# Cached values with the probabilities as the stationary operand, loaded ahead of the scans, in a two-layer hybrid decoder step

## The chip, the cores and the metric

One core of one Trainium2 chip runs the whole program. The metric is the device time of one execution in microseconds (us). The kernel before takes 2830.28 us (median of three runs, 2822.64 to 2831.82). TensorE is called PE, its weight loads PEld, VectorE DVE, ScalarE ACT, GpSimd POOL; SP only issues transfers.

## The reference

Two layers are run on 520 tokens: a prompt of 512 tokens and 8 sample tokens, each sample with a cache of 1024 positions, held as 8 pages of 128 positions that a page table points to. Per layer:

```
x = x + rms_post(Mix(rms_pre(x)))
x = x + rms_post2(ConvFFN(rms_pre2(x)))
```

`Mix` projects the normalised input once (29 tiles of 128 columns, and 32 tiles of gate logits) and feeds four branches: A, sparse attention (an indexer picks the top 256 of the 1025 keys of a sample, the top 128 of those of the prompt; 4 query heads, 2 key/value heads of 64), B, stick-breaking attention (4 heads of 64), C, an mLSTM scan, and D, a Mamba-2 scan. For a sample token, A and B need the products of 1024 cached probabilities and cached values for each head:

```
o = einsum('btjgn,btnjd->btjgd', p, v_sel)     # A, the selected ones, others have p = 0
o = einsum('bhtl,blhd->bthd', a, v)            # B
```

Each branch is projected, multiplied by the sigmoid of its gate logits and summed. `ConvFFN` follows with 44 up tiles and 22 down tiles.

## The kernel before, in words

**The ring.** Weights and cached pages come through four slots `R`. SP issues them in the order of the list `TILES`, and `tile_used` counts the tiles that PE is done with; a slot is loaded again when the tile four before is used. A cached unit is two pages: of keys 128 x 512 floats each (A's keys, two of B's, and the indexer's keys in 64 rows with zeros below), of values 128 x 384 each (128 of A, 256 of B). For each page the issuing engine first reads the page number out of `PT` into a register (`value_load`) and then issues the transfer (L403, L404, `cached`).

**The order in a layer.** First come 12 projections (L497), then the key stage (32 units; `rec` at L637 to L647): for each unit PE multiplies the indexer's queries `QI` (64 rows), A's queries `QA` (128 rows) and twice B's queries `QB` (128 rows) with the pages, each with 32 stationary columns and 256 moving ones, into partitions 0, 32 and 64. SP issues the units' pages and ACT those of the odd units from the fifth on. Then 17 projections, between which DVE selects the top 256 of the samples and PE, ACT and DVE do the other small steps. Then, in this order:

- sample probabilities of A transposed (L680, L682), copied by ACT into `PA` (L1079); 
- 12 groups of features turned token-major (PE L695, `TO_TM`), with ACT's evacuations (L1097) and the convolutions of D between them (DVE L1318, L1315); 
- cumulative sums (L706), row terms (L713), sample gates (L720), dots (L725 to L728), and eight steps for the samples' states (PE L742 and L746, POOL L1749 and L1755, DVE); 
- the scans of C and D: eight heads `v`, each with four blocks of key-query products (L776, L779), a broadcast (L758), decays on ACT (L1164, L1166), diagonals and weights on POOL, a product on DVE, and the state and output products on PE (L787 to L808);
- four blocks `t` of prompt queries for A and B (L842 to L895): the indexer's scores, the top-k on DVE for `t` of 1 to 3, softplus and sums for B, softmax for A.

**The fill.** The 32 gate tiles have no consumer before the branches are merged, so PE computes them (L582) in between. A step is 3 matmuls of 128 x 260, 16 steps are one tile. `fill(upto)` on PE, `drain(upto)` on ACT (which copies each half tile into `RB`, L1021) and `follow(upto)` on POOL run up to a given number of steps: `PRE` for the places ahead of the scans (96 steps), `LOOP` for the eight heads (64) and `IN_T`/`TO_T` for the four query blocks (352). SP stores each half from `RB` (L447, `keep`), and ACT may write `RB` again when the store has landed.

**Cached values before.** In head `v` of the scans PE multiplies the pages of sample `v` (L557, L562, `cached_values`), after the four key-query blocks of that head. The page is stationary, 128 x 128, and the probabilities move: 4 columns for A, 2 for each of B's two pairs. `MIX` puts the 32 value units into the list of tiles, four before each head's gate tiles, so they go through the ring:

```
mm(PS[:, 7, 448 + 4 * b:448 + 4 * b + 4], slot(l, n)[:, v0:v0 + 128],
   PA[:, 32 * j + 4 * b:32 * j + 4 * b + 4], start=j == 0, stop=j == 7,
   skip_group_check=True)
```

After the scans DVE adds and places the results (L1609 to L1617, signal `sa_out`), and PE waits for that in the first query block.

Of the kernel before, what the change touches and what calls it, by code (L numbers as in the profile page):

```python
# [11 lines left out]
NPR = 512  # L12
NSM = 8
TOK = NPR + NSM
HALF = TOK // 2
# [5 lines left out]
PAGES = 8  # L21
# [62 lines left out]
PRE = [0, 32, 48, 64, 72, 80, 96]  # L84
LOOP = [96 + STEPS * (v // 2 + 1) for v in range(8)]
SPENT = LOOP[-1]
IN_T = [[24, 16, 28, 12], [24, 16, 32, 14], [24, 16, 38, 14], [24, 16, 42, 12]]
TO_T = [[SPENT + sum(map(sum, IN_T[:t])) + sum(IN_T[t][:p + 1]) for p in range(4)] for t in range(NT)]
assert TO_T[-1][-1] == STEPS * NG

MIX = [("gate", q) for q in range(PRE[-1] // STEPS)]
for v in range(8):
    MIX += [("V", UPS * v + t) for t in range(UPS)]
    MIX += [("gate", q) for q in range((LOOP[v - 1] if v else PRE[-1]) // STEPS, LOOP[v] // STEPS)]
MIX += [("gate", q) for q in range(SPENT // STEPS, NG)]
TILES = ([("proj", c) for c in range(CUT)] + [("K", u) for u in range(NU)]
         + [("proj", c) for c in range(CUT, NPROJ)] + MIX + [("br", d) for d in range(KD)]
         + [("out", d) for d in range(KD)] + [("up", j) for j in range(2 * JF)] + [("down", t) for t in range(JF)])
AT = {tile: n for n, tile in enumerate(TILES)}

SPLIT_NEXT = [[q + 2] if AT["gate", q + 2] == AT["gate", q] + 2 else [] for q in range(NG - 2)] + [[], []]
IN_LOOP = [list(range((LOOP[v - 1] if v else PRE[-1]) // STEPS, LOOP[v] // STEPS)) for v in range(8)]
IN_LOOP[7] += [LOOP[7] // STEPS, LOOP[7] // STEPS + 1]
assert sorted([0, 1] + sum(SPLIT_NEXT, []) + sum(IN_LOOP, [])) == list(range(NG))

# [14 lines left out]
def trunk_kernel(nc, x_in, pages, consts, vecs, states, c_state, d_state, k_c, v_c,  # L120
# [9 lines left out]
    with ctx:  # L130
# [48 lines left out]
        QI = sb("QI", [64, NSM, 32])  # L179
# [4 lines left out]
        PA = QB[:, :, :, :].rearrange("p c b h -> p (c b h)")  # L184
# [30 lines left out]
        tile_used = sig("tile_used", NPROJ + 2 * NU + 40 + 8 + 44 + 22)  # L215
# [103 lines left out]
        sa_own = sig("sample_a_own_value", 1)  # L319
        sa_out = sig("sample_a_output", 1)  # L320
# [36 lines left out]
        for l in range(L):  # L357
            for n in range(tiles_per):
                at[(l * tiles_per + n) % RING] += 32 if TILES[n][0] in ("K", "V") else 16
                full_at.append(at[(l * tiles_per + n) % RING])  # L360
# [38 lines left out]
        def cached(eng, l, n, u, rec, src):  # L399

            eng.wait_ge(tile_used.sem, l * tiles_per + n - RING + 1)
            for j in range(2):
                pg = eng.value_load(PT[0:1, 2 * u + j:2 * u + j + 1], min_val=0, max_val=POOL - 1)  # L403
                eng.dma_start(slot(l, n)[:, rec * j:rec * (j + 1)],  # L404
                              src[l, bass.ds(pg, 1)].rearrange("o p c -> (o p) c")).then_inc(full(l, n)[0], 16)
# [5 lines left out]
        def _(sp):  # L411
# [14 lines left out]
            for l in range(L):  # L426
# [8 lines left out]
                for u in range(NU):  # L435
                    if not by_act(u):
                        cached(sp, l, AT["K", u], u, K_REC, k_c)
# [3 lines left out]
                def keep(n):  # L441

                    if TILES[n][0] == "gate":
                        q = TILES[n][1]
                        for a in range(2):
                            sp.wait_ge(*g_out.nth(l, 2 * q + a))
                            sp.dma_start(GATES[l, q, :, HALF * a:HALF * (a + 1)],  # L447
                                         RB[:, HALF * a:HALF * (a + 1)]).then_inc(g_stored[a].sem, 16)
                for kind, i in MIX:
                    n = AT[kind, i]  # L450
                    if kind == "V":
                        cached(sp, l, n, i, V_REC, v_c)
                    else:
                        tile(l, n, w_gate[l, i], 1024)
                    keep(n - RING)
# [1492 lines left out]
```

## Time and profile before

| what | value |
|---|---|
| median of three runs | 2830.28 us (2822.64 to 2831.82) |
| the profiled execution, its own time | 2841.91 us |
| its span, first to last instruction | 2839.8 us |
| mean granted clock of TensorE | 0.895 of full |
| PE busy | 89% of the span |
| DVE, ACT, POOL busy | 45%, 36%, 12% |
| DMA | 264.0 MB, 93 GB/s on the mean |

The page of the profile gives the busy time of each engine and the costliest groups of instructions. PEclk is the granted clock of TensorE as a share of its full speed (2.4 GHz; 0.5 is the lower level, 1.2 GHz). An idle time in brackets says how long the engine had been idle before the row, and who released it. Matmuls overlap, so the cost of one is read from start to start of neighbours rather than from its duration. The two layers are alike; a stage of the first one begins some 1407 us before that of the second.

### The profile page before, as it was taken

The page shows a single profiled execution, that of the slowest core. Times are in us where ns is not written, and L with a number is a line of the kernel's source. Part 1 is how long each engine was busy: PE and PEld are TensorE (multiplying, and loading weights), DVE is VectorE, ACT ScalarE, POOL GpSimd, SP SyncE. Part 2 cuts the span into 40 slices and gives each one's busy share as a digit, 9 for nine tenths or more (in the row PEclk, how much of TensorE's full clock was granted, in tenths as well). Part 3 has the DMA queues.
Part 4 walks back from the last instruction along what each step waited for, and adds up shares of the span by engine and source line. Part 5 has one row for each costly group of instructions (what it writes and reads, how often), then busy time and mean ns, then how long its engine had stood idle before and what let it go on. Part 6 is the DMA issues. An engine that isn't in the chain of part 4 may idle for free. (4 is left out here: it accounts for less than half of the span.)

```text
span 2839.8 us, 41630 instructions
## 1 busy us (share of the span) xinstructions
PE 2540.2 (89%) x16456; PEld 2175.6 (77%) x16456; DVE 1285.4 (45%) x2047; ACT 1013.4 (36%) x1526; POOL 348.1 (12%) x390
## 2 busy tenths in 40 slices
PE   6999679989999889999888997899899997999996
PEld 5659657767887789999885686477687776999895
DVE  3329341223556465662342383422234565666623
ACT  3123431224444345552230225222244433555521
POOL 0014232112320000000000132311222100000000
PEclk9999766769999899999999997676799998999998
DMA  3362112232326122222314422122322251222221
GB/s 151 111 201 90 58 47 77 77 100 68 89 75 196 60 67 91 97 91 82 103 60 148 156 75 68 58 68 83 92 79 89 84 172 52 83 97 90 88 84 60
DMA packets 111827, 264.00 MB, mean 93 GB/s; under 512 B 13458, under 2 KB 47250, under 8 KB 110738
## 3 DMA queue, kind: packets, MB, share of 16 engines
q1 hardware_dynamic: 99074, 238.25, 26.4%
q10 hardware_dynamic: 12560, 23.11, 2.4%
q8 instruction: 130, 2.13, 0.3%
q14 instruction: 63, 0.52, 0.1%
HBM read 233.71 MB, written 27.59 MB: 92 GB/s over the span
## 5 line engine op out<-in xcount | busy, mean ns | idle before, releaser
L497 PE MATMUL PS<-XH,WH 128*128 128x260 f32 x2592 | 540.2, 290 | 47.9 <-DVE XL L1315 36.3
L1003 ACT ACTIVATE WH<-R 128x1024 fp32r<-128x1024 f32 x270 | 286.0, 1059 | 780.5 <-PE PS L497 564.9
L497 PE MATMUL PS<-XL,WH 128*128 128x260 f32 x2592 | 529.2, 286 | 4.3 <-issue 2.8
L497 PE MATMUL PS<-XH,WL 128*128 128x260 f32 x2592 | 528.1, 285 | 0.0
L1339 DVE TENSOR_TENSOR WL<-R,WH 128x1024 fp32r<-128x1024 f32 x176 | 215.7, 1226 | 555.9 <-ACT WH L1003 555.6
L497 PEld LDWEIGHTS PS<-XH,WH 128*128 128x128 f32 x2592 | 408.6, 193 | 56.7 <-issue 43.7
L497 PEld LDWEIGHTS PS<-XL,WH 128*128 128x128 f32 x2592 | 406.3, 192 | 4.7 <-issue 4.7
L497 PEld LDWEIGHTS PS<-XH,WL 128*128 128x128 f32 x2592 | 405.7, 192 | 0.0
L582 PE MATMUL PS<-XH,WH 128*128 128x260 f32 x1024 | 304.8, 298 | 16.5 <-ACT RB L1021 16.3
L1714 POOL TENSOR_TENSOR WL<-R,WH 128x1024 fp32r<-128x1024 f32 x94 | 223.3, 2376 | 730.8 <-ACT WH L1003 729.9
L582 PE MATMUL PS<-XL,WH 128*128 128x260 f32 x1024 | 298.3, 291 | 0.0
L582 PE MATMUL PS<-XH,WL 128*128 128x260 f32 x1024 | 297.0, 290 | 0.0
L582 PEld LDWEIGHTS PS<-XH,WH 128*128 128x128 f32 x1024 | 202.4, 198 | 29.9 <-issue 22.2
L582 PEld LDWEIGHTS PS<-XH,WL 128*128 128x128 f32 x1024 | 202.1, 197 | 0.0
L582 PEld LDWEIGHTS PS<-XL,WH 128*128 128x128 f32 x1024 | 202.0, 197 | 0.0
L497 PE MATMUL PS<-FR,WH 128*128 128x260 f32 x1024 | 190.8, 289 | 8.9 <-issue 8.9
L497 PEld LDWEIGHTS PS<-FR,WH 128*128 128x128 f32 x1024 | 154.4, 195 | 9.7 <-issue 9.7
L1318 DVE SCALAR_TENSOR_TENSOR S<-S,V 128x510 f32<-128x510 f32 (+1 forms) x176 | 132.1, 751 | 44.9 <-ACT S L1282 41.8
L1021 ACT ACTIVATE RB<-PS 128x260 f32<-128x260 f32 x128 | 49.6, 387 | 246.8 <-PE PS L582 144.7
L915 PE MATMUL PS<-F,R 128*128 128x260 f32 x512 | 119.4, 388 | 4.5 <-DVE F L1315 3.1
L915 PEld LDWEIGHTS PS<-F,R 128*128 128x128 f32 x512 | 94.4, 190 | 29.1 <-DVE F L1315 9.8
L562 PE MATMUL PS<-QB,R 128*128 128x2 f32 x512 | 113.0, 325 | 0.0
(311 smaller groups left out, 3398.9 us busy)
## 6 DMA issues: line engine op xcount, KB each, us to landing
R<-w_up SPq DMA_DIRECT2D x88, 512.0 KB, 3.3
R<-w_gate SPq DMA_DIRECT2D x64, 512.0 KB, 3.7
R<-w_proj SPq DMA_DIRECT2D x58, 512.0 KB, 3.3
R<-v_c SPq DMA_DIRECT2D x128, 192.0 KB, 2.4
R<-w_down SPq DMA_DIRECT2D x44, 512.0 KB, 3.2
R<-k_c SPq DMA_DIRECT2D x72, 256.0 KB, 3.3
GATES<-RB SPq DMA_DIRECT2D x128, 130.0 KB, 3.7
S<-GATES SPq DMA_DIRECT2D x64, 260.0 KB, 2.7
```

Of the source, the lines that this page charges most:

```text
L497: i = mm(PS[:, bank + a, 0:HALF], p[:, w, k * 128:(k + 1) * 128], x[:, a * HALF:(a + 1) * HALF], start=first and p is WH and x is hi, stop ...
L562: ins = mm(PS[:, 7, o:o + 2], slot(l, n)[:, v0 + 128 + 128 * c:v0 + 256 + 128 * c], PA[:, 256 + 32 * j + 4 * b + 2 * c:256 + 32 * j + 4 * ...
L582: i = mm(PS[:, 1 + 2 * a, 0:HALF], p[:, half(l, m), k * 128:(k + 1) * 128], x[:, k, a * HALF:(a + 1) * HALF], start=k == 0 and p is WH and ...
L915: ins = mm(PS[:, 4 + 2 * (q % 2) + a, 0:HALF], slot(l, nb)[:, 256 * br + 128 * k:256 * br + 128 * k + 128], F[:, o + k, a * HALF:(a + 1) * ...
L1003: do(A(WH[:, half(l, m), :], slot(l, SPLIT[m]), ACT.Copy), w_hi)
L1021: do(A(RB[:, HALF * a:HALF * (a + 1)], PS[:, 1 + 2 * a, 0:HALF], ACT.Copy), g_out)
L1318: do(v_.scalar_tensor_tensor(out, a, sc, b, o0, o1), s)
L1339: v_.tensor_tensor(WL[:, half(l, m), :], slot(l, SPLIT[m]), WH[:, half(l, m), :].bitcast(f32), ALU.subtract).then_inc(w_lo.sem, 1)
L1714: g_.tensor_tensor(WL[:, half(l, m), :], slot(l, SPLIT[m]), WH[:, half(l, m), :].bitcast(f32), ALU.subtract).then_inc(w_lo_p.sem, 1)
```

## The change

The pages of values become the moving operand and the probabilities the stationary one. Four samples are handled side by side: for page `j` of samples `4 s` to `4 s + 3` (a quad, `k = 8 s + j`, 16 in a layer) PE issues four matmuls with 8 stationary columns and 384 moving ones, into partitions 0, 32, 64 and 96 of bank 0 or 2. Each matmul gives all 8 rows of probabilities (4 heads of A, 4 of B) against all 384 value columns, of which a head wants its own 64. ACT copies the bank out (`values_out`), PE picks the rows and turns them feature-major with three matmuls (`by_feature`), and DVE places the wanted parts. `PA` is laid out again, 8 probabilities of a page and sample side by side.

The quads do not pass the ring. They have two buffers of their own, `QUAD[0]` in `S` and `QUAD[1]` in the room of `TM` that D's features fill later; SP issues the four pages of quad `k` when quad `k - 2` is used. The first two quads are used after step 24 of the fill, and two more after each of the first seven token-major groups. `MIX` is gone: the gate tiles follow each other in the ring.

The fill is dealt out anew: 192 steps ahead of the samples' states (16 before A's sample probabilities are transposed, 12 behind each of seven token-major groups, and others), 4 in each of the eight state steps, 8 in each of the eight heads, and 224 in the query blocks. The exponential for A's samples moves behind the last projection. In the key stage `QI` has 128 rows, the lower 64 zeros, so that all four matmuls have the same shape.

The diff, cut to its core:

```
-PRE = [0, 32, 48, 64, 72, 80, 96]
-LOOP = [96 + STEPS * (v // 2 + 1) for v in range(8)]
-IN_T = [[24, 16, 28, 12], [24, 16, 32, 14], [24, 16, 38, 14], [24, 16, 42, 12]]
+LAST, PAST_P = 16, 24
+IN_TM = [36, 48, 60, 72, 84, 96, 108, 112, 120, 128, 136, 144]
+CUM, ROWS, SEL, DOTS = 160, 176, 184, 192
+IN_R = [DOTS + 4 * (s + 1) for s in range(8)]
+LOOP = [IN_R[-1] + 8 * (v + 1) for v in range(8)]
+IN_T = [[14, 10, 12, 10], [14, 10, 18, 12], [14, 10, 22, 14], [14, 10, 26, 14]]
...
+NQ = 16
+QUADS_AT = [PAST_P, PAST_P] + [IN_TM[i] for i in range(7) for _ in range(2)]
+LOAD_QUADS = [[k for k in range(NQ) if (QUADS_AT[k - 2] // STEPS + RING - 1 if k >= 2 else 1) == q] for q in range(NG)]
...
-        QI = sb("QI", [64, NSM, 32])
+        QI = sb("QI", [128, NSM, 32])
...
+        PA = QB[:, :, :, :].rearrange("p c b h -> p (c b h)").rearrange("p (n h) -> p n h", h=8)
+        QUAD = [buf[:, 0:4 * V_REC].rearrange("p (g c) -> p g c", g=4)
+                for buf in (S[:, 2:5, :].rearrange("p a t -> p (a t)"),
+                            TM[:, T_XX:T_XX + 4, :, :].rearrange("p a t d -> p (a t d)"))]
...
+                def cached_values(k):
+                    s, j = divmod(k, PAGES)
+                    if k == 0:
+                        sp.wait_ge(*sb_a.nth(l, 0))
+                    elif k >= 2:
+                        sp.wait_ge(*quad_used.nth(l, k - 2))
+                    for g in range(4):
+                        sp.dma_start(QUAD[k % 2][:, g, :],
+                                     v_c[l, bass.ds(page(sp, PAGES * (4 * s + g) + j), 1)].rearrange("o p c -> (o p) c")
+                                     ).then_inc(quad_full[k % 2].sem, 16)
+                for q in range(NG):
+                    tile(l, AT["gate", q], w_gate[l, q], 1024)
+                    if q >= RING:
+                        keep(q - RING)
+                    for k in LOAD_QUADS[q]:
+                        cached_values(k)
...
+            def cached_values(l, k):
+                s, j = divmod(k, PAGES)
+                pe.wait_ge(quad_full[k % 2].sem, 64 * (NQ // 2 * l + k // 2 + 1))
+                for g in range(4):
+                    ins = mm(PS[32 * g:32 * g + 8, 2 * s, 0:V_REC], PA[:, PAGES * j + 4 * s + g, :], QUAD[k % 2][:, g, :],
+                             start=False, stop=j == PAGES - 1, skip_group_check=True)
+                finish(ins, quad_used)
+            def by_feature(l, s):
+                pe.wait_ge(*sv_copied.nth(l, s))
+                pick = ident.rearrange("p (g r) -> p g r", g=4)
+                mm(PS[:, 2 * s, 384:400].rearrange("p (g h) -> p g h", g=4), PST[:, 0:128], pick[:, :, 0:4],
+                   start=True, stop=True)
+                for c in range(2):
+                    o = 400 + 8 * c
+                    ins = mm(PS[:, 2 * s, o:o + 8].rearrange("p (g h) -> p g h", g=4),
+                             PST[:, 128 + 128 * c:256 + 128 * c], pick[:, :, 4 + 2 * c:6 + 2 * c], start=True, stop=True)
+                finish(ins, sv_out)
...
-                    mm(PS[0:32, bank, col:col + 256], QI[:, b, :], rec[0:64, 3], start=st, stop=end,
+                    mm(PS[0:32, bank, col:col + 256], QI[:, b, :], rec[:, 3], start=st, stop=end,
...
+                fill(LAST)
                 pe.wait_ge(*sa_p.nth(l, 0))
...
+                fill(PAST_P)
                 pe.wait_ge(*sa_trc.nth(l, 0))
                 pe.wait_ge(*sa_own.nth(l, 0))
+                cached_values(l, 0)
+                cached_values(l, 1)
...
                     finish(ins, tm_done)
+                    fill(IN_TM[i])
+                    if i < 7:
+                        cached_values(l, 2 * i + 2)
+                        cached_values(l, 2 * i + 3)
+                    if i in (4, 9):
+                        by_feature(l, i // 5)
...
                         finish(ins, st_block)
-                    cached_values(l, v)
-
                     pe.wait_ge(*vu_ready.nth(l, v))
...
+                pe.wait_ge(*sa_out.nth(l, 0))
                 for i, c in enumerate([CQ, CQ + 1, CK, CK + 1, XC, XC + 1, XB, XB + 1]):
...
+                def values_out(s):
+                    act.wait_ge(*quad_used.nth(l, PAGES * s + PAGES - 1))
+                    if s:
+                        act.wait_ge(*sv_out.nth(l, 0))
+                    do(A(PST[:, 0:V_REC], PS[:, 2 * s, 0:V_REC], ACT.Copy), sv_copied)
...
+                    drain(IN_TM[i])
+                    if i in (3, 8):
+                        values_out(i // 5)
...
+                for s in range(2):
+                    dve.wait_ge(*sv_out.nth(l, s))
+                    o = OS[:, 16 * s:16 * s + 16]
+                    tt(o, o, PS[:, 2 * s, 384:400], ALU.add)
...
```

The four fills of a query block stand after the first products of A (`IN_T[t][0]`), after the sums of B (`[1]`), after the values of B (`[2]`) and after the last products of A (`[3]`).

## Rows read from the trace of the kernel before

**Rows 1.** The page of the profiled execution, busy times of the engines.

```profile
PE 2540.2 (89%) x16456; PEld 2175.6 (77%) x16456; DVE 1285.4 (45%) x2047; ACT 1013.4 (36%) x1526; POOL 348.1 (12%) x390
```

**Rows 2.** Busy times by stage, second layer: length, each engine, PEclk, DMA share, GB/s.

```profile
1522.00:1590.30 68.30, 60.08 (x290) 19.05 (x290) 0.50 (x3) 1.11 (x2) 0.00 (x0) 0.93 0.74 237
1709.00:1814.30 105.30, 76.52 (x414) 58.74 (x412) 50.03 (x96) 46.01 (x76) 28.02 (x17) 0.73 0.20 63
1749.00:1790.00 41.00, 27.23 (x182) 26.08 (x184) 10.45 (x36) 17.56 (x32) 7.89 (x6) 0.79 0.24 74
1790.00:1814.30 24.30, 20.49 (x32) 5.58 (x28) 21.06 (x19) 5.42 (x7) 13.00 (x9) 0.54 0.09 27
1814.30:2018.00 203.70, 190.84 (x860) 142.54 (x860) 39.76 (x60) 47.25 (x67) 43.42 (x102) 0.69 0.27 81
2036.00:2264.00 228.00, 220.62 (x1408) 181.83 (x1406) 103.54 (x261) 100.42 (x180) 57.96 (x56) 0.95 0.27 80
```

**Rows 3.** Same view, the eight stretches of cached values in the scans, second layer.

```profile
1828.36:1838.69 10.33, 10.33 (x50) 10.31 (x49) 0.46 (x2) 1.06 (x1) 2.88 (x3) 0.50 0.37 106
...
sum 71.37, PE 71.37 PEld 71.25 DVE 4.85 ACT 22.73 POOL 19.81; mean PE 8.92 PEld 8.91 DVE 0.61 ACT 2.84 POOL 2.48
```

**Rows 4.** Timeline of PE in the second stretch of cached values: start, duration, what.

```profile
1855.73 0.39 PE L557 MATMUL PS<-QB,R 128*128 128x4 f32 x2
...
1856.42 0.36 PE L557 MATMUL PS<-QB,R 128*128 128x4 f32 x2
...
1857.41 0.57 PE L557 MATMUL PS<-QB,R 128*128 128x4 f32 x2
...
1858.69 0.57 PE L557 MATMUL PS<-QB,R 128*128 128x4 f32 x2
```

**Rows 5.** The chain that ended last, second layer: start, duration, what.

```profile
1952.18 3.98 PE PS L803 x8
...
1957.34 5.88 PE PS L582 x48
...
2064.93 2.30 PE PS L879 x8
```

**Rows 6.** Timeline of PE, one unit of the key stage, first layer.

```profile
126.35 0.62 PE L637 MATMUL PS<-R,QI 64*32 64x256 f32 x2
126.90 0.40 PE L639 MATMUL PS<-R,QA 128*32 128x256 f32 x1
126.90 0.40 PE L647 MATMUL PS<-R,QB 128*32 128x256 f32 x1
...
127.88 0.62 PE L637 MATMUL PS<-R,QI 64*32 64x256 f32 x2
```

**Rows 7.** Busy times in the middle of the key stage, first layer.

```profile
130.00:180.00 50.00, 44.28 (x234) 14.60 (x233) 0.00 (x0) 0.00 (x0) 0.00 (x0) 1.00 0.86 275
```

**Rows 8.** Who PE waited for ahead of the scans, second layer: total, times, longest.

```profile
PE PS L706 <- DVE SMT L1315: 8.7, 1, 8.7
```

**Rows 9.** The same view inside the scans, second layer.

```profile
PE PS L758 <- DVE S L1315: 8.8, 3, 3.5
```

**Rows 10.** Timeline of SP's queue: two key pages; three value pages across two units.

```profile
1560.44 1.43 SPq L404 DMA_DIRECT2D R<-k_c  x2
...
1834.37 2.90 SPq L404 DMA_DIRECT2D R<-v_c  x3
```

**Rows 11.** DMA issues of cached pages: count, KB each, median us to landing.

```profile
R<-v_c SPq DMA_DIRECT2D x128, 192.0 KB, 2.4
```

**Rows 12.** Timelines of POOL, PE and DVE, last query block, second layer.

```profile
2217.39 1.37 POOL L1708 TENSOR_SCALAR_AFFINE_SELECT F<-F 128x128 f32<-128x128 f32 x4 [8.18 <-DVE F L1318]
...
2219.31 1.02 PE L866 MATMUL PS<-F,K 128*128 128x512 f32 x2
...
2245.41 0.15 DVE L1321 TENSOR_SCALAR MX<-MX 128x1 f32<-128x1 f32 x1
...
2250.81 1.98 PE L857 MATMUL PS<-F 64*128 64x512 f32 x4
```

More of the change, by code:

```diff
@@ L214, in trunk_kernel @@
         slot_full = [sig(f"slot{i}_full", 0) for i in range(RING)]
-        tile_used = sig("tile_used", NPROJ + 2 * NU + 40 + 8 + 44 + 22)
+        tile_used = sig("tile_used", NPROJ + NU + 40 + 8 + 44 + 22)
+        quad_full = [sig(f"value_pages{i}_loaded", 0) for i in range(2)]
+        quad_used = sig("value_pages_used", NQ)
         xt_ready = sig("normalised_ready", 16)
@@ L436, in _ @@
                     if not by_act(u):
-                        cached(sp, l, AT["K", u], u, K_REC, k_c)
+                        cached_keys(sp, l, u)
                 for c in range(CUT, NPROJ):
                     tile(l, proj(c), w_proj[l, c], 1024)
[L441 to L455, printed above, removed]
+                def keep(q):
+                    for a in range(2):
+                        sp.wait_ge(*g_out.nth(l, 2 * q + a))
+                        sp.dma_start(GATES[l, q, :, HALF * a:HALF * (a + 1)],
+                                     RB[:, HALF * a:HALF * (a + 1)]).then_inc(g_stored[a].sem, 16)
@@ L709, in _ @@
                 finish(ins, sm_cum)
-                fill(PRE[3])
+                fill(CUM)
                 pe.wait_ge(*sm_rt.nth(l, 0))
@@ L714, in _ @@
                 finish(ins, sm_tr)
-                fill(PRE[4])
+                fill(ROWS)
                 pe.wait_ge(*xbc_ready.nth(l, 5))
@@ L722, in _ @@
                 finish(ins, r_sel)
-                fill(PRE[5])
+                fill(SEL)
                 pe.wait_ge(*r_prod.nth(l, 0))
@@ L730, in _ @@
                 finish(ins, r_tr)
-                fill(PRE[6])
+                fill(DOTS)
                 for s in range(8):
@@ L748, in _ @@
                     finish(ins, r_bc)
+                    fill(IN_R[s])
                 pe.wait_ge(*sm_em.nth(l, 0))
@@ L1109, in _ @@
                     token_major(c)
-                token_major(7)
-                drain(PRE[1])
-                for i in range(8, len(TO_TM)):
+                for i in range(7, len(TO_TM)):
                     token_major(i)
-                drain(PRE[2])
                 act.wait_ge(*sm_v.nth(l, 0))
@@ L1149, in _ @@
                 do(A(S[0:8, 3, 0:512], PS[0:8, 2, :], ACT.Copy), r_trc)
-                drain(PRE[6])
+                drain(DOTS)
+                for s in range(8):
+                    drain(IN_R[s])
                 for c in range(2):
@@ L1733, in follow @@
                     while STEPS * (behind[0] + 1) <= upto:
-                        for nxt in SPLIT_NEXT[behind[0]]:
-                            split_rest(l, NPROJ + nxt)
+                        if behind[0] + 2 < NG:
+                            split_rest(l, NPROJ + behind[0] + 2)
                         behind[0] += 1
-                follow(PRE[4])
+                follow(DOTS)
                 pool.wait_ge(*r_trc.nth(l, 0))
```

119 lines of the change are left out of this document (45 added, 74 removed).

## The prediction

> **What bounds the kernel now.** The page comes first: PE is busy for 89% of the span, DVE for 45% [rows 1]. So PE's own work is the time, and an edit counts when it takes PE work out or moves PE's waits. Next come the busy times by stage [rows 2]: in the second layer the key stage lasts 68.3 us, the stretch ahead of the scans 105.3, the scans 203.7 and the query blocks 228.0. The reader is to see three things. PE is full in the scans (190.8 of 203.7) but granted 0.69 of its clock. Ahead of the scans it idles for 29 us, 8.7 of them in one wait for the log decays [rows 8]. In the query blocks it is full at 0.95. The changed instructions fill eight stretches of the scans, 71.4 us in all [rows 3], and the first of them runs at a granted clock of 0.50.
>
> The timeline shows why they are dear: a page (six records) takes 0.69 us from start to start while the clock is still full, and 1.28 us when it has fallen [rows 4]. Each record loads 128 columns for 2 or 4 moving ones. Here row and rule differ. By the Trainium skill, "TensorE: Matmul & The Clock Gate", section "LDWEIGHTS (loading the stationary operand)", 128 columns load in an estimated 107 ns. With it the 384 records of a layer would cost 41 us and the change would be worth 30 us less in a layer. The trace agrees at full clock alone (0.69 / 6 = 115 ns); at the lower level it shows 213 ns. I take the 71.4 us that were measured.
>
> **Prices.** A fill step is 5.88 us / 16 = 0.37 us [rows 5]. A record of 256 moving columns beside a partner in another column group is (127.88 - 126.90) / 4 = 0.245 us, and the two partners start in the same 10 ns [rows 6]. So a record of 384 columns is 0.37 us, and a quad (two records, four groups side by side) 0.73 us; one after another it would be 2.9 us. Four groups at once are not shown; two are, so I take 0.73. SP's two pages back to back take 1.43 us, the second issue itself 0.33, so 1.10 us from page to page; three pages across a unit's wait take 2.90, so 1.47 for the one behind the wait [rows 10]. A quad costs SP 4 x 1.10 + 0.37 = 4.8 us, and a gate's tile and two stores are three more issues of 0.33 us and a little, 1.25 us together. A page lands 2.4 us after its issue [rows 11].
>
> **The scans.** Out go 71.4 us. PE waits 8.8 us for DVE in three places [rows 9]; two of them (3.5 each) lie in heads that had no fill behind them and now have 8 steps: 5.8 less. In two heads (v = 2 and 4) the fill halves from 16 steps to 8 and no longer covers ACT's root and DVE's reciprocal ahead of the next product: 2.4 more each, 4.8, my estimate. Clock: the output products take 3.98 us behind a cached stretch and 2.30 for the same columns in the query blocks [rows 5]; eight heads could give 13 us there and some more on the small ones, but heads with waits fall back, so I take 10. The fill stays 64 steps. Sum -82, between -62 (no clock gain, all waits opened) and -95.
>
> **Ahead of the scans.** The fill grows from 96 to 224 steps here. In order:
> - To the second quad: 24 steps 8.8, transposes and the opening of two banks 2, two quads 1.5: 12.3 us.
> - The seven groups with two quads each. PE's own work is 84 steps 30.9, 14 quads 10.2, transposes and picking 6.6: 47.7 us. SP has 14 quads at 4.8 (66.8) and five gates at 1.25 (6.3), and the last landing 2.4: 75.5 us. With two buffers SP can't run ahead: quad k waits for quad k - 2. So **SP's issuing sets the pace**, 10.8 us for a group, and PE idles some 3 us in each. Behind the waiting SP stand the gate stores and gate tiles; the tiles have a ring of four and the stores a gate's length, so I add nothing. The bytes are no bound: 1.6 MB in 10.8 us is 146 GB/s, beside 275 in the key stage [rows 7].
> - Five more groups: 36 steps 13.2, the rest 5: 18.2.
> - From the decays to the dots: 48 steps as before, and the 8.7 us wait stays, since ACT starts that chain when the fill ahead of it is drained. 41, as in the trace [rows 2].
> - The state steps took 24.3 us, DVE busy for 21.1 of them [rows 2]; 32 steps (11.8) lie in their gaps in part: 32.
>
> Sum 179 against 105: +74. The bounds are +46 (SP costs nothing) and +84 (quads one after another, which makes PE's group 11 us and adds waits). ACT's two copies, DVE's 18 small placings and the move of A's exponential lie behind fills of 16 steps and more: 0; if that cover fails it is about 3 us.
>
> **Query blocks.** 128 steps fewer: -47. But the fills covered other work. In the last block POOL's mask ends at 2217.39 + 1.37 = 2218.76 and PE takes it at 2219.31, and DVE's chain before POOL is fixed [rows 12]. With 10 steps fewer (3.7 us) PE waits 3.1 us. Over four blocks this point gives some 10 us, the second fill (6 steps fewer against a slack near 1.2) 4, and in the last block the maximum is ready at 2245.6 while PE, which came at 2250.81, would now come near 2243: 2.5. So +16, sum -31, between -20 and -47.
>
> **Key stage.** The index products, of another shape, run alone for 0.55 us of a unit's 1.53 [rows 6]. With 128 rows they can join the others: 0.98. But the transfers are 86% busy at 275 GB/s in the middle of the stage [rows 7], and 28 units of 0.52 MB take 53 us at that rate. I take -5, between -13 (DMA always busy) and +10 (the gaps let the clock fall, and a unit takes twice 0.98).
>
> **The sum.** -82 + 74 - 31 - 5 = -44 us in a layer, -88 in two. The profiled execution took 2841.9 us (span 2839.8), which is 11.6 above the median of the runs; 2841.9 - 88 = 2754, and against the median **2742 us**.
>
> **The rivals.**
> - *SP's issuing is hidden.* Then the seven groups take PE's 47.7 us, 28 less in a layer: 2686. This is what a rule gives too. By the Trainium skill, "DMA: Bandwidth & Descriptors", section "Issuing engines are not separate DMA queues", the sequencer's time to start a DMA is usually small beside the DMA. Against it: at 275 GB/s a page of 0.197 MB needs 0.7 us and SP 1.10 [rows 7, 10]. For it: PE's waits let SP catch up. 0.12.
> - *The scans give back only the matmuls.* The clock stays low in heads full of small products and the waits open: 62 instead of 82, 2782. For it: 0.69 of the clock now [rows 2]. 0.17.
> - *Quads one after another.* 10 us more in a layer, 2762. Against it: the pair that starts together [rows 6]. 0.10.
> - *The key stage doesn't pack.* Its part of the change does nothing: 2752. 0.06.
> - *Slower: the idle times ahead of the scans and in them drop the clock for all fills there.* 288 steps at 0.71 us instead of 0.37 cost 98 us in a layer, of which SP's pace hides 28; the 10 us of clock gain go too. That is +80, so 2902 us. It decides from the point where over half of these steps run slow (44 of 80). Against it: the stretch ahead of the scans idled for 29 us and still had 0.73 [rows 2]. 0.06.
>
> The forecast has 0.49, with a range of its own of 2710 to 2775. The cases between 2675 and 2795 hold 8 in 10, once the bounds of the scans and of the groups are taken in; outside lie the slower case and the far ends. About 0.3% (8 us) is what a measurement can tell from no change. Faster 0.91, within it 0.03 (part of the clock case), slower 0.06.
>
> **What would show it.** Right: no PE rows of 128x2 and 128x4 in the scans, that stage near 120 us; in the groups SP's page rows 1.1 us apart without gaps, and PE waiting about 3 us for them in each; four rows of 8 columns that start together; new waits of 1 to 3 us ahead of L866's counterpart; the key stage near 60 us with DMA its main wait. Wrong: a stretch ahead of the scans of about 150 us (SP hidden) or over 200; a scan stage over 140; fills at 0.71 us a step through whole groups; or index products that still start alone.

## The result, and the profile after

The changed kernel takes **2884.0 us** in the median of four runs (2878.9 to 2886.5) where the kernel before takes 2830.7: 1.9% slower, a ratio of 1.0192 with a 95% interval of 1.0168 to 1.0217. The forecast was 2742. The profiled execution took 2882.1 us with a span of 2878.8; that is 39 us over the span of before, whose profiled execution was itself 11 us above its median.

First the page's busy times, for [rows 1].

```profile
PE 2418.3 (84%) x15976; PEld 2059.0 (72%) x15976; DVE 1289.5 (45%) x2065; ACT 1015.8 (35%) x1530; POOL 347.9 (12%) x390
```

PE has 122 us less to do, and the kernel is slower: over 160 us of idle time are new. The stages of the second layer say where (busy times by stage, for [rows 2]: key stage; all that lies ahead of the scans; of it the seven groups and the state steps; scans; query blocks. Columns: length, PE, PEld, DVE, ACT, POOL, PEclk, DMA share, GB/s).

```profile
1545.90:1607.40 61.50, 42.37 (x290) 18.18 (x290) 0.00 (x0) 0.00 (x0) 0.00 (x0) 0.80 0.78 254
1726.70:1929.20 202.50, 153.29 (x943) 120.72 (x943) 55.20 (x118) 58.48 (x98) 49.00 (x26) 0.78 0.40 118
1739.50:1820.00 80.50, 57.17 (x417) 43.10 (x417) 22.34 (x40) 25.17 (x43) 11.85 (x5) 0.83 0.65 187
1881.70:1929.20 47.50, 41.40 (x129) 24.65 (x129) 18.13 (x20) 2.22 (x4) 16.09 (x11) 0.61 0.06 17
1929.20:2080.20 151.00, 110.06 (x454) 66.09 (x453) 40.01 (x57) 50.27 (x71) 38.96 (x100) 0.75 0.07 21
2098.80:2303.00 204.20, 176.30 (x1029) 135.38 (x1027) 102.00 (x260) 86.63 (x158) 39.04 (x48) 0.95 0.18 57
```

| stage of a layer, us | before | forecast | after |
|---|---|---|---|
| key stage (mean of both layers) | 66.3 | 61.3 | 64.0 |
| seven groups with quads | - | 75.5 | 80.5 |
| the rest ahead of the state steps | - | 71.5 | 74.5 |
| state steps | 24.3 | 32 | 47.5 |
| scans | 203.7 | 122 | 151.0 |
| query blocks | 228.0 | 197 | 204.2 |

The stages from the state steps on hold most of the error: 15.5 us in the state steps, 29 in the scans, 7 in the blocks. (The last 8 of the scans' 64 fill steps, 3 us, lie behind the end of this stage in the changed kernel and inside it in the kernel before, so like for like the scans take 154 us.) The waits of PE name the places. Who PE waited for in the scans, for [rows 9], and then in the state steps (total, times, longest):

```profile
PE PS L811 <- DVE F L1350: 18.8, 4, 9.0
PE PS L808 <- DVE F L1350: 17.4, 3, 9.0
PE PS L790 <- ACT F L1201: 3.8, 1, 3.8
...
PE PS L773 <- POOL F L1785: 6.3, 1, 6.3
PE PS L777 <- POOL F L1791: 6.1, 1, 6.1
```

The wait of 6.3 us ahead of L773 ends at 1881.74, just where the state steps begin; the one of 6.1 lies in them. In the scans PE waits 6 to 9 us in every other head. Three of these four waits (7 to 9 us) stand where a gate has just ended; the fourth, 6.0 us in the first head, has another cause (POOL itself waits there 7.7 us for ACT's decays) and is there in the kernel before too, with 5.1 us ahead of L776, in a line of the view of [rows 9] that is not shown there. DVE is only the last link; the timeline of all engines at one of the three places has the first (start, duration, engine and line, operation; in brackets the idle time before and who ended it).

```profile
2021.53 1.06 ACT L1031 ACTIVATE WH<-R 128x1024 fp32r<-128x1024 f32 x1
2022.74 2.34 POOL L1750 TENSOR_TENSOR WL<-R,WH 128x1024 fp32r<-128x1024 f32 x1 [33.19 <-ACT WH L1031]
2025.15 1.38 POOL L1744 TENSOR_SCALAR_AFFINE_SELECT F<-F 128x128 f32<-128x128 f32 x4
2026.60 0.92 POOL L1805 COPY U<-F 128x1 f32<-128x1 f32 x4
2027.62 2.06 POOL L1807 TENSOR_SCALAR S<-TM,U 128x64 f32<-128x64 f32 x4
2029.77 1.27 DVE L1350 TENSOR_TENSOR F<-F,PS 128x512 f32<-128x512 f32 x2 [9.41 <-POOL S L1807]
2030.51 1.65 PE L811 MATMUL PS<-F 128*128 128x256 f32 x4 [8.98 <-DVE F L1350]
```

It is read from the bottom. PE's third block (L811) waits for DVE's product, DVE for POOL's weights (L1807). POOL had stood idle for 33.19 us: the next item in its queue was the low part of a gate's weights (L1750), which needs ACT's leading part (L1031), and ACT makes that only when PE has ended the gate two before. So the order is: fill ends, ACT copies and splits, POOL makes the low part (2.34), and only then the next head's diagonals and weights (4.5), DVE, PE. In the kernel before, POOL's queue had the same order, a low part ahead of the next head's weights, and POOL idled for 27 us ahead of it. There ACT made the leading part as soon as the gate's tile had landed, in the middle of a head, under 10 us of cached values [rows 3] and with a fill still to come. POOL and DVE at such a place of the kernel before:

```profile
1890.26 2.34 POOL L1714 TENSOR_TENSOR WL<-R,WH 128x1024 fp32r<-128x1024 f32 x1 [27.09 <-ACT WH L1003]
1895.13 2.05 POOL L1770 TENSOR_SCALAR S<-TM,U 128x64 f32<-128x64 f32 x4
...
1909.42 1.27 DVE L1315 TENSOR_TENSOR F<-F,PS 128x512 f32<-128x512 f32 x2
```

The next head's weights are done at 1897.18, and DVE's product comes 12 us later. The change takes the cover away and ties the leading part to the end of a fill.

**Theory 1**: POOL's queue, as told. **Theory 2**: the fills run at a low clock in the state steps and scans (0.61 and 0.75), and PE would be the bound there even without the waits. **Theory 3**: SP's issuing sets the seven groups.

### The profile page after: what moved, and what is told of

Same layout as the page of the kernel before. It is cut to its first block and busy times, and to the rows that moved or that the text cites. A ratio compares the mean times of both kernels' runs of the same rounds, so it can differ in the third digit from the quotient of the medians.

```text
span 2878.8 us, 40698 instructions
## 1 busy us (share of the span) xinstructions
PE 2418.3 (84%) x15976; PEld 2059.0 (72%) x15976; DVE 1289.5 (45%) x2065; ACT 1015.8 (35%) x1530; POOL 347.9 (12%) x390
## 5 line engine op out<-in xcount | busy, mean ns | idle before, releaser
L514 PE MATMUL PS<-XH,WH 128*128 128x260 f32 x2592 | 540.4, 290 | 46.9 <-DVE XL L1350 35.1
L1031 ACT ACTIVATE WH<-R 128x1024 fp32r<-128x1024 f32 x270 | 286.0, 1059 | 723.6 <-PE PS L514 567.7
L514 PE MATMUL PS<-XL,WH 128*128 128x260 f32 x2592 | 528.4, 285 | 3.5 <-ACT WH L1031 3.5
L514 PE MATMUL PS<-XH,WL 128*128 128x260 f32 x2592 | 528.9, 286 | 0.0
L514 PEld LDWEIGHTS PS<-XH,WH 128*128 128x128 f32 x2592 | 409.2, 193 | 55.5 <-issue 44.1
L514 PEld LDWEIGHTS PS<-XL,WH 128*128 128x128 f32 x2592 | 405.8, 191 | 3.9 <-issue 3.9
L514 PEld LDWEIGHTS PS<-XH,WL 128*128 128x128 f32 x2592 | 406.5, 192 | 0.0
L601 PE MATMUL PS<-XH,WH 128*128 128x260 f32 x1024 | 319.4, 312 | 28.5 <-ACT RB L1049 24.6
L1750 POOL TENSOR_TENSOR WL<-R,WH 128x1024 fp32r<-128x1024 f32 x94 | 223.5, 2378 | 900.8 <-ACT WH L1031 899.7
L601 PE MATMUL PS<-XL,WH 128*128 128x260 f32 x1024 | 307.7, 300 | 0.0
L601 PE MATMUL PS<-XH,WL 128*128 128x260 f32 x1024 | 306.3, 299 | 0.0
L601 PEld LDWEIGHTS PS<-XH,WH 128*128 128x128 f32 x1024 | 212.0, 207 | 66.9 <-issue 53.8
L601 PEld LDWEIGHTS PS<-XL,WH 128*128 128x128 f32 x1024 | 212.1, 207 | 0.0
L601 PEld LDWEIGHTS PS<-XH,WL 128*128 128x128 f32 x1024 | 211.9, 207 | 0.0
L1353 DVE SCALAR_TENSOR_TENSOR S<-S,V 128x510 f32<-128x510 f32 (+1 forms) x176 | 132.1, 751 | 44.3 <-ACT S L1317 40.9
L656 PE MATMUL PS<-R,QI 128*32 128x256 f32 x128 | 53.7, 532 | 52.1 <-DMA R<-k_c 42.5
```

What stands on the lines that cost most here:

```text
L514: i = mm(PS[:, bank + a, 0:HALF], p[:, w, k * 128:(k + 1) * 128], x[:, a * HALF:(a + 1) * HALF], start=first and p is WH and x is hi, stop ...
L601: i = mm(PS[:, 1 + 2 * a, 0:HALF], p[:, half(l, m), k * 128:(k + 1) * 128], x[:, k, a * HALF:(a + 1) * HALF], start=k == 0 and p is WH and ...
L656: mm(PS[0:32, bank, col:col + 256], QI[:, b, :], rec[:, 3], start=st, stop=end, skip_group_check=True)
L1031: do(A(WH[:, half(l, m), :], slot(l, SPLIT[m]), ACT.Copy), w_hi)
L1353: do(v_.scalar_tensor_tensor(out, a, sc, b, o0, o1), s)
L1750: g_.tensor_tensor(WL[:, half(l, m), :], slot(l, SPLIT[m]), WH[:, half(l, m), :].bitcast(f32), ALU.subtract).then_inc(w_lo_p.sem, 1)
```

## The experiments

### One thing in another order (e1_late_rest)

POOL makes a gate's low part one step or one head later, behind the next head's weights. The gate needs it 16 fill steps on, so nothing new waits.

```
-                follow(DOTS)
+                follow(SEL)
...
-                    follow(IN_R[s])
+                    follow(IN_R[s - 1] if s else DOTS)
...
-                    follow(LOOP[v])
+                    follow(LOOP[v - 1] if v else IN_R[7])
+                follow(LOOP[7])
```

> Edit: POOL makes a gate's low part (2.35 us) one head, or one state step, later: behind the next head's weights in place of ahead of them. Nothing else differs from the changed kernel (2884 us). Theory 1 (POOL's queue: the low part stands ahead of the next head's diagonals and weights, so the state products come about 9 us after the fill): PE's waits in the scans of the second layer for VectorE and ACT (18.8 + 17.4 + 3.8) fall under 15 together and the stage goes from 151 to about 120 us; the state steps lose their two waits of 6 us and go from 47.5 to 38 to 44; together 35 to 40 us in a layer, so 2804 to 2815 us. Theory 2 (the low clock of the fills in these stages, the waits are only where the slack shows): PE stays the bound there, the fills slow down as the waits go, less than 12 us in a layer, so over 2860 us. Theory 3 (SP's issuing in the groups): no difference, 2884.

Measured: **2785.9 us**, 98 less than the changed kernel and 0.9842 of the kernel before (0.9794 to 0.9889). Busy times of its state steps and scans, second layer, and what is left of PE's waits in the scans:

```profile
1820.50:1858.90 38.40, 35.42 (x128) 21.94 (x128) 17.92 (x19) 2.22 (x4) 18.49 (x12) 0.69 0.13 38
1858.90:1981.30 122.40, 103.57 (x454) 61.90 (x453) 39.23 (x58) 50.28 (x71) 39.00 (x100) 0.82 0.09 26
```

```profile
PE PS L808 <- DVE F L1350: 8.4, 2, 6.0
PE PS L790 <- ACT F L1201: 6.3, 1, 6.3
PE PS L811 <- DVE F L1350: 3.1, 2, 2.6
```

The scans take 122.4 us, the state steps lose 9 and the dots ahead of them 4 (the wait of 6.3 us falls to 1.7). These are 42 us in a layer, the other 7 are spread over quads, key stage and blocks; I had expected 35 to 40 in all. One reason: the granted clock of the scans rises from 0.75 to 0.82 as the waits go, and PE's busy time falls by 6.5 us for the same instructions. In the state steps 6.0 of the 9 us are PE's busy time, at 0.61 before and 0.69 now. What is left of the waits that were to fall under 15 us is 17.8; 12.3 of it stand in the first head, the 6.0 us ahead of L808 from above and 6.3 ahead of L790, and are no matter of POOL's order. The same place as above, in this kernel:

```profile
1942.98 0.92 PE L811 MATMUL PS<-F 128*128 128x256 f32 x4
1943.06 1.06 ACT L1031 ACTIVATE WH<-R 128x1024 fp32r<-128x1024 f32 x1
...
1944.26 2.35 POOL L1750 TENSOR_TENSOR WL<-R,WH 128x1024 fp32r<-128x1024 f32 x1 [11.78 <-ACT WH L1031]
```

POOL does the same 2.35 us at the same moment, but PE is past L811 already. Theory 1 holds.

### The fill in the state steps (e9_no_state_fill, e7_late_no_state_fill)

The 32 fill steps of the state steps go to the query blocks, with the low part where the change has it, and with it late.

```
-IN_R = [DOTS + 4 * (s + 1) for s in range(8)]
+IN_R = [DOTS] * 8
...
+IN_T = [[18, 12, 14, 10], [18, 12, 20, 12], [18, 12, 24, 14], [18, 12, 28, 14]]
```

> Edit: the changed kernel (low part where it was, ahead of the next head's weights) without fill in the state steps, their 32 steps in the query blocks. With the late low part this moved the state steps from 38 to 28 us, the scans from 122 to 115 and gave 28 us in all (2786 to 2758). If the two causes (POOL's order, fill at half clock in the state steps) are independent: the state steps fall from 47 to about 28 (both waits of 6 us are gone with the fill as well), the scans stay at 143 to 151, the blocks take 2 to 8 more, 2840 to 2855 us. If the state steps' waits come back in the scans' first heads: over 2860.

> Edit: the low part a head later, and no fill in the eight state steps: their 32 steps go to the query blocks, 8 to each. In the run with the late low part alone the state steps take 38.4 us and the fill there runs at half clock (2.9 us for four steps). If the fill at half clock is what makes them long: the steps fall to the 24 of the kernel before, 14 less, and the blocks take 32 x 0.37 = 12 more less the 3 to 8 us of waits that they cover: 2770 to 2785 us. If the clock of the state steps costs nothing beyond their work, no gain: 2786 or more.

| time, us | fill in the state steps | none |
|---|---|---|
| low part as in the change | 2884.0 | 2822.3 |
| low part late | 2785.9 | 2757.6 |

The two causes are not independent: the late low part gives 98 us with this fill in place and 65 without it. e9 is at 0.9968 of the kernel before (0.9952 to 0.9983), 18 us better than the best that I expected: its state steps fall from 47.5 to 25.5 us and the scans from 151 to 145.7, and the blocks take 205.4 in place of 204.2. e7 is at 0.9733 (0.9694 to 0.9773), 12 us under the range expected of it: the state steps fall to 28.2 and 28.1 us (24 expected), and the scans give 6 and 10 more, the 10 in the second layer, where PE's wait of 6.3 us ahead of L790 is gone. In e1 ACT had stood at the state steps' last gate copy and split, with the output gates and the first head's decays behind it. Why the fill is dear there is in the groups of instructions of the changed kernel, the fill's leading product first in the state steps, then in the scans (count, busy, mean ns):

```profile
L601 PE MATMUL PS<-XH,WH 128*128 128x260 f32 x32 | 13.5, 423 | 0.0
...
L601 PE MATMUL PS<-XH,WH 128*128 128x260 f32 x57 | 16.9, 296 | 0.0
```

One takes 423 ns there against 296. From start to start it is plainer: in six of the eight state steps the four fill steps take 2.8 us together (0.70 a step), in the other two 1.6 (0.39). The state steps' own products (8 rows, 512 columns) keep PE busy for 22.4 of 25.5 us at a granted clock of 0.50 without any fill (e9), and most of the fill put in between runs at the lower level too. The 32 steps, 12 us at the 0.37 of [rows 5], cost 22 us of the stage in the changed kernel (POOL's wait of 6.1 included) and 10 in e1; in the blocks e7 pays 3 and 5.5 us for them. Theory 2 is right of this one stage; of the scans it is not (122 us with the fill in place).

### The seven groups (e3_loads_once, e2_static_pages)

In e3 the first two quads alone are loaded and PE multiplies them again in place of the other fourteen; in e2 the page numbers are constants and the look-up in the page table is left out. e3 first, then e2:

```
-                        sp.wait_ge(*quad_used.nth(l, k - 2))
+                        return
...
-                pe.wait_ge(quad_full[k % 2].sem, 64 * (NQ // 2 * l + k // 2 + 1))
+                pe.wait_ge(quad_full[k % 2].sem, 64 * (l + 1))
```

```
-                                     v_c[l, bass.ds(page(sp, PAGES * (4 * s + g) + j), 1)].rearrange("o p c -> (o p) c")
+                                     v_c[l, PAGES * (4 * s + g) + j]
```

> Edit: only the first two quads of each layer are loaded, and PE multiplies these again for the other fourteen (the values of the other pages are left out). PE's work is unchanged, SP issues 8 pages in a layer in place of 64. It gives what PE's own pace in the groups is: by my sum 47.7 us at full clock (84 fill steps, 14 quads, the transposes). Theory 3: the groups take 48 to 52 us and the kernel 2820 to 2830 us; what static page numbers leave over this is landing and transfer. If the clock of the groups is what holds them: over 60 us.

> Edit: the pages of cached values have constant numbers, so SP reads no register for them; the look-up in the page table is left out for the values, the bytes and the waits are the same. Theory 3 (SP's issuing at 1.10 us a page sets the pace of the seven groups): a page costs SP about 0.33 us and a quad 1.3 to 1.7, the groups go from 80.5 us to between 50 and 58, 22 to 30 us in a layer, 2824 to 2840 us. If the landing of the transfers (2.4 us behind each wait for a buffer) sets it with two buffers, the groups stay over 70 us, 2865 or more. If PE's own work at a lower clock sets it, they also stay over 70, with PE busy for over 90% of them.

e3: 2814.2 us. Without loads the quads' stretch takes 46.3 us, all of it PE, at full clock (I had 47.7). e2: 2841.2 us. Busy times of that stretch, second layer, e3 and then e2:

```profile
1702.00:1748.30 46.30, 46.30 (x416) 36.77 (x415) 22.42 (x40) 25.22 (x43) 11.91 (x5) 1.00 0.30 87
```

```profile
1721.90:1776.70 54.80, 47.74 (x416) 36.10 (x416) 22.39 (x40) 25.17 (x43) 11.87 (x5) 1.00 0.84 274
```

SP's queue, in the changed kernel and then in e2 (start, duration, pages in a row):

```profile
1763.13 3.64 SPq L465 DMA_DIRECT2D S<-v_c  x4
1767.55 3.63 SPq L465 DMA_DIRECT2D TM<-v_c  x4
```

```profile
1751.55 1.76 SPq L465 DMA_DIRECT2D S<-v_c  x4
1753.54 1.75 SPq L465 DMA_DIRECT2D TM<-v_c  x4
```

Four pages take SP 3.64 us with a number read from the table, 1.1 apart as forecast, and 1.76 without. The loads cost 34 us in a layer over PE's own pace: in the second layer PE's idle time is 23 of them, and the other 11 are the same PE work at a granted clock of 0.83 in place of 1.00. SP's look-ups are a bound: without them 17 us of the first layer's 34 go and 26 of the second's (the stretches take 63.5 and 54.8 us), which is the total gain of 43. The rest, 17 and 9 us, stays with static numbers; these runs do not say how much of it is SP's shorter issues, transfer or landing.

### Sharing the pages (e5, e6, e10, e12, e13, e14)

If SP is the bound, another queue should help. None gave what was expected.

> Edit: the low part a head later (as in the run of 2786 us), and ACT issues two of the four pages of twelve quads in each layer, right behind its copy of a group's transposes; SP issues the other two. The run with pages loaded once gave 37 us a layer in the groups, so what is left to win is at most 74 us. Theory 3 (issuing): SP's quad falls from 4.8 to 2.6 us, and ACT's 4.4 us of issues a group fit beside its 7 us of other work or just not: groups 62 to 72 us in place of 80, 2735 to 2765 us. Rival (ACT is full in the groups: its evacuations come later, and PE waits for them in place of the pages): groups over 75 us, 2775 or more.

> Edit: as the run before it in this call, but ACT issues one page of a quad and SP three. Theory 3: SP's quad costs 3 x 1.10 + 0.37 = 3.7 us, 16 in a pair with its gate parts near 8.5 us a group in place of 10.8, about as long as PE's own 8.3: groups 62 to 68 us, 2725 to 2755 us. If ACT is the limit, one page is better than two by over 10 us; if SP is, two are better than one.

> Edit: low part late, no fill in the state steps (2758 us), and POOL issues two of the four pages of the quads from the third on, right behind its own wait for the buffer; SP issues the other two. ACT's issues came late, since they stood behind its copies in order; POOL is free there. Theory 3 (the pace is wait for the buffer, issues one after another, landing, twice in a group): 62 to 70 us in place of 79 in the quads, 2724 to 2740 us. Rival (POOL's way of making a DMA's descriptors costs more than SP's, or it slows DVE by the port they share): quads over 76, 2752 or more.

| kernel | pages by SP + other | base, us | us | quads' stretch, layers 1, 2 |
|---|---|---|---|---|
| e1 | 4 | - | 2785.9 | 77.0, 78.9 |
| e5 | 2 + 2 ACT | 2785.9 | 2785.6 | 76.6, 81.2 |
| e6 | 3 + 1 ACT | 2785.9 | 2776.0 | 74.5, 74.7 |
| e7 | 4 | - | 2757.6 | 79.0, 79.7 |
| e10 | 2 + 2 POOL | 2757.6 | 2752.5 | 78.5, 76.9 |

Only e6 is worth more than 5 us, 9.9 or 0.4%, and its runs (2769.6 to 2781.9) overlap with those of e1 (2773.9 to 2790.8). ACT reached its pages behind its copies, POOL behind a gate's low part. Three runs more start from e11 of the last section below (2737.5 us, quads 79.9 and 77.0): e12 has POOL issue two pages of a quad and moves its low part behind both quads' pages, e13 takes the gate stores out of SP's queue (ACT issues them), e14 does both.

> Edit: as the run of 2737.5 us (low part late, no fill in the state steps, 16 steps more in the groups), and POOL issues two of the four pages of each quad from the third on; other than in the first such run, its low part of a gate stands behind the pages of both quads of a group, not between them. There POOL's 2.4 us of low part stood ahead of the second quad's pages (1702.07 to 1704.47, the page at 1705.69) and the quads took 77 us all the same. Theory 3 with POOL's order as in theory 1: 62 to 70 us for the quads, 2705 to 2725 us. Rival (with two buffers that come free together, wait, issue, transfer and landing follow one another, so halving the issues gives little): quads over 74 us, 2733 or more.

> Edit: as the run of 2737.5 us (low part late, no fill in the state steps, 16 steps more in the groups), and the two stores of a gate leave SP's queue: ACT issues them right behind its own copies. Is SP bound by the sum of its issues (two quads 9.6, a gate's tile and stores 1.25 a group), the stores' 0.9 us go: 10.8 to 9.9 us a group, quads 71 to 74 us, 2722 to 2730 us. Is it the chain (both buffers come free together; wait, eight pages, landing), the stores are beside it: quads 76 to 80 us, 2733 to 2742.

> Edit: the run before it, and POOL issues two pages of each quad, its low part behind both quads' pages. In the run with SP's stores (2739 us) one group took 8.2 us and the next 12.6: there the first half of a gate was copied at 1709.57 and the second at 1712.44, behind a store that SP issued late. If SP's order (a gate's stores behind waits for free page buffers) holds the groups once the issues are shared: all groups take 8 to 9 us, quads 60 to 66 us, 2700 to 2715 us. If transfer and landing of eight pages after one wait hold them, or ACT is now late: quads over 74 us, 2733 or more.

e12: 2739.3 us, quads 82.0 and 84.8. e13: 2734.4, quads 81.1 and 80.8; the sum of SP's issues alone is not what decides. Its 3 us on e11 lie within the spread of the runs; its blocks are shorter (190.7 us against 196.1 in the second layer), its quads longer. e14: 2738.9, quads 81.5 and 83.8. ACT's, POOL's and PE's rows of e14 in one group:

```profile
1704.86 0.39 ACT L1049 ACTIVATE RB<-PS 128x260 f32<-128x260 f32 x1 [2.43 <-PE PS L601]
...
1705.70 1.06 ACT L1031 ACTIVATE WH<-R 128x1024 fp32r<-128x1024 f32 x1 [0.46 <-ACT RB L1049]
```

```profile
1702.51 0.55 POOL L1779 DMA_DIRECT2D TM<-v_c  x1 [0.63 <-issue]
1705.88 0.54 POOL L1779 DMA_DIRECT2D TM<-v_c  x1 [2.82 <-issue]
1706.43 2.36 POOL L1752 TENSOR_TENSOR WL<-R,WH 128x1024 fp32r<-128x1024 f32 x1
```

```profile
1708.89 0.56 PE L601 MATMUL PS<-XH,WH 128*128 128x260 f32 x1 [4.07 <-issue]
```

PE's last fill product ends at 1704.82 and the next starts at 1708.89, just when the low part is done (1708.79): now the page issues stand ahead of it. It is theory 1's pattern the other way round: PE's waits for pages (19 us in e13's second layer) fell to 2.3, and 22 us of idle time ahead of the fill took their place. What POOL's page at 1705.88 waited for over its 2.82 us the trace does not name. Whether the groups could come near e2's 55 us with shared queues in the right order stays open.

### The key stage (e4_key64)

The index operand back to 64 rows.

> Edit: the index operand of the key stage back to 64 rows, all else as in the changed kernel. If the packing works and is worth something, the key stages of the two layers (66.4 and 61.5 us) become longer, up to the 64.3 and 68.3 of the kernel before: 0 to 7 us in a layer, 2884 to 2896 us, and the index products start 0.5 us ahead of the other two again. If the stage is bound by its transfers either way, no difference beyond 3 us: 2884. If the idle times of the packed form cost more clock than they give, it is faster: 2875 to 2880.

Measured: 2886.0 us (2884.3 to 2890.2), no difference from 2884.0. Busy times of its two key stages; those of the changed kernel took 66.4 and 61.5 us:

```profile
118.70:182.40 63.70, 58.15 (x289) 18.67 (x290) 0.00 (x0) 0.32 (x1) 0.00 (x0) 0.95 0.77 245
1543.80:1606.40 62.60, 57.41 (x290) 18.53 (x290) 0.00 (x0) 0.22 (x1) 0.00 (x0) 0.97 0.78 250
```

Timeline of PE in the changed kernel: three products do start together.

```profile
122.19 0.63 PE L666 MATMUL PS<-R,QB 128*32 128x256 f32 x1
122.20 0.63 PE L656 MATMUL PS<-R,QI 128*32 128x256 f32 x1
122.20 0.63 PE L658 MATMUL PS<-R,QA 128*32 128x256 f32 x1
```

The packing takes 15 us of PE's busy time out of each stage (58 and 57 to 43 and 42), the granted clock falls from 0.95 and 0.97 to 0.81 and 0.80, and the stage is as long as with 64 rows: PE's waits for pages grow from 5.0 to 19.1 us in the second layer, and the pages arrive at 245 to 254 GB/s in both forms. The part is worth nothing. The kernel before took 68.3 us in its second layer; as e4 takes 62.6 with the same products, that difference is not the packing's, and its cause is open.

### Fill where PE waits anyway (e8, e11)

e8 moves 16 steps from the state steps into the groups (with the late low part), e11 moves 16 from the blocks into them (with no fill in the state steps).

> Edit: the low part a head later, 16 steps moved from the state steps (two in each in place of four) into the first seven groups, where PE waits for pages that SP issues. Theory 3: the groups do not get longer (PE's own 8.3 us and 0.9 for two more steps are under SP's 10.8), the state steps lose 16 x 0.5 = 8 us or so, 2765 to 2775 us. If the groups are bound by PE at a low clock in part, they take 6 us more, and the time stays at 2780 to 2790.

> Edit: low part late, no fill in the state steps, and 16 steps moved from the query blocks into the seven groups, where PE waits for pages. In the run before, 16 steps more in the groups made them no longer (78.3 and 80.5 us against 77.0 and 78.9: 1.5 more). Theory 3: groups + 0 to 2 us, blocks -2 to -6 us: 2745 to 2758 us. If the blocks give nothing back (their waits grow as the fill goes): 2757 to 2762.

e8: 2779.7 us (2777.7 to 2790.7), 6 less than e1 and within the spread of the two, which is less than theory 3 had promised; the groups grow by 1.5 us in each layer. e11: **2737.5 us** (2734.6 to 2747.3), 20 less than e7 where I had expected at most 12: groups 79.9 and 77.0 us with 16 steps more in them, blocks 198.0 and 196.1 in place of 205.4 and 208.5. Where it comes from shows in the busy times of the quads' stretch, second layer, e7 and then e11:

```profile
1672.80:1752.50 79.70, 57.92 (x416) 43.80 (x416) 22.31 (x40) 25.17 (x43) 11.81 (x5) 0.83 0.64 189
```

```profile
1666.60:1743.50 76.90, 59.23 (x464) 46.47 (x463) 23.13 (x40) 26.64 (x45) 14.17 (x6) 0.91 0.69 202
```

With 48 products more PE is busy for only 1.3 us more, as the granted clock rises from 0.83 to 0.91. In the blocks PE's busy time falls by 10.7 us, of which the 16 steps are 5.9; there the clock goes from 0.93 to 0.96.

With e13's stores the time is 2734.4, the lowest of all, at 0.9653 of the kernel before (0.9636 to 0.9671), 3.5% faster: the change pays once the fill and POOL's queue are fitted to it. No run gives the kernel before a new deal of its fill or ACT's stores, so how much of the 3.5% the stationary probabilities themselves are worth stays open.

## Why the prediction was wrong

- **The step that failed** is the sum of the scans, in "PE waits 8.8 us for DVE in three places" and what follows: it priced DVE's and ACT's latencies behind a shorter fill and never looked at POOL's queue. The low part stood ahead of the next head's weights in both kernels; the change moves its making from the middle of a head, under 10 us of cached values, to the end of a fill, with nothing between it and PE's need. The waits were put at -1 us (5.8 less, 4.8 more) and the clock at -10; measured, PE's idle time in the scans grew by 28 us (12.9 to 40.9) and its busy time for the work that stayed fell by 6 (119.5 to 113, the last 8 fill steps counted in). The order cost 29 us in a layer there, and 9 in the state steps and 4 ahead of them: with the late low part the kernel takes 98 us less, over two thirds of the error of 142.
- State steps: 32 forecast, 47.5 measured. About 9 of the difference went with the late low part; the other 6 were the price of the fill, which I had put at 0.37 us a step "in the gaps in part", and of which most ran at the lower level, at 0.70 us a step.
- Once POOL's order is mended, the scans' -82 is nearly right: like for like e1 gives -78 (203.7 to 125.4, the last 8 fill steps counted in). Two misses cancel in part: PE's idle time grew by 6 us in place of falling by 1, and the clock gave 13 in place of 10. The waits that were priced came close (7.8 less, against 5.8; 5.1 more behind root and reciprocal, against 4.8); the one left out is that of 6.3 us in the first head, which the fill in the state steps brings.
- Groups: the 1.1 us from page to page was right, and so was PE's own 47.7 (46.3); 80.5 against 75.5. That SP's issues alone set the pace is shown in part: static numbers take 17 and 26 of the 34 us away, and fewer pages on SP shortened the stage by 4 us at most (e6). The sum held PE at full clock, and it ran at 0.83. The rival "SP's issuing is hidden" does not hold: a page costs SP 1.10 us where its 0.197 MB need 0.7 at the 275 GB/s of [rows 7]. The Trainium skill says in "DMA: Bandwidth & Descriptors", section "Issuing engines are not separate DMA queues", that the sequencer's time to start a DMA is usually small beside the DMA; this trace does not agree.
- Quads one after another: refuted. In e3's trace the four records of a pass start at 337.170, 337.177, 337.183 and 337.190, the next four from 337.497 on, and the next quad 0.65 us behind the first: a quad is 0.65 us of PE at full clock, against my 0.73.

```profile
337.17 0.83 PE L570 MATMUL PS<-S,QB 128*8 128x384 f32 x8
337.82 0.51 PE L570 MATMUL PS<-TM,QB 128*8 128x384 f32 x4
```

- Key stage: -5 forecast, nothing by e4; the transfers are the bound, as [rows 7] would have allowed.
- Query blocks: -31 forecast, -24 measured. The waits for POOL's mask that I had put at 10 us in four blocks measured 10.8; I had left out those for ACT: its gate copy (8.0 us, 2.0 in the kernel before) and L872 (6.8, 1.9 before).
- The slower rival had the sign and not the cause: it wanted the clock of all fills at half; the fills in the scans measure 296 ns a product, near full clock. A rival of the right sign, a queue whose order turns against its reader, was missing altogether, and so 0.91 for faster was far too sure.

## What to carry to other kernels

When work that covered a chain is taken out, write down for every in-order queue (the idle ones first: POOL was busy for 12%) what stands ahead of the next critical instruction, and what that in turn waits for. An item that is needed 16 steps from now does not belong ahead of one that is needed next; making one kind of item a step or a head later was worth 98 us here. And put filling work where the engine waits for something slow: in the groups 16 steps more raised the granted clock and cost PE 1.3 us of busy time; in a chain of small steps most of them ran at the lower level, at 0.70 us each.

## What the runs showed of the hardware

- A DMA whose page number is read from a table costs SP 1.1 us from issue to issue; one with a constant number 0.48 ((1.76 - 0.33) / 3, with 0.33 for an issue itself).
- Four records of 8 stationary and 384 moving columns, in four column groups, start within 20 ns of each other (e3), and the next four 0.33 us after the first.
- The same fill product took 296 ns in the scans and 423 in the state steps of one kernel; e1's scans ran at a granted clock of 0.82 with fewer waits, the changed kernel's at 0.75. From the one to the other the waits listed fall by 22 us (41.0 to 18.8) and the stage by 29.
- Work taken out of a stage that is bound by transfers came back as idle time and a lower clock: 15 us less PE work, 0.96 to 0.80 in the mean, the same length (64 us; 63 with 64 rows).
